# RWKV core stage: 26 products a round in place of 30, with wider ones, on sequences copied by GpSimd

## The reference, cut to what matters

```
def rwkv7_step(S, inp):
    r_t, dec_t, k_t, v_t, kk_t, a_t = inp
    sa = jnp.einsum('bhij,bhj->bhi', S, -kk_t)
    S = (S * dec_t[:, :, None, :]
         + sa[..., None] * (kk_t * a_t)[:, :, None, :]
         + v_t[..., None] * k_t[:, :, None, :])
    y = jnp.einsum('bhij,bhj->bhi', S, r_t)
    return S, y
```

## Time and profile before

| | |
|---|---|
| median of 3 runs | 2794.38 us (2792.1 to 2809.73) |
| the profiled execution | 2812.66 us, its span 2810.9 us |
| PE busy | 2584.5 us of the span (92%), 26234 matmuls |
| DVE, ACT, POOL busy | 1440.3, 1164.2, 947.7 us |
| core stage | 281.3 to 505.0 us: 223.7 us, PE busy 171.9 us |

### The profile page before, as it was taken

One profiled execution on the slowest core, in us unless ns is written; L12 is line 12 of the kernel. 1 busy time (PEld: TensorE's weight loads), 2 busy tenths in 40 slices (PEclk: granted clock), 3 DMA queues, 4 the chain that ended last, 5 costly groups with the idle time before them and its releaser, 6 DMA issues.

```text
span 2810.9 us, 64105 instructions
## 1 busy us (share of the span) xinstructions
PE 2584.5 (92%) x26234; PEld 2414.1 (86%) x26234; DVE 1440.3 (51%) x2006; ACT 1164.2 (41%) x1683; POOL 947.7 (34%) x392
## 2 busy tenths in 40 slices
PE   6797777798999999999899999999999899999997
PEld 5776777488799999988697999999998758999997
DVE  7827444421267774389654677743143234655521
ACT  7732333444343443333544434434246533543432
POOL 2232000044144445433441444444442202444442
PEclk8798999999999999999999999999999889999999
DMA  3121000124122223322221223233222101222231
GB/s 136 61 68 49 16 4 5 65 84 141 46 83 97 90 90 106 124 79 82 91 91 43 85 97 97 90 106 113 89 90 68 46 0 54 97 90 95 99 103 63
DMA packets 61128, 219.96 MB, mean 78 GB/s; under 512 B 6688, under 2 KB 7072, under 8 KB 60320
## 3 DMA queue, kind: packets, MB, share of 16 engines
q1 hardware_dynamic: 57536, 206.43, 21.8%
q10 hardware_dynamic: 3424, 11.01, 1.0%
HBM read 213.22 MB, written 4.19 MB: 77 GB/s over the span
## 4 chain that ended last, share of the span: by engine, by line
PE 64%; issue 22%; DVE 8%; POOL 3%; ACT 3%; DVEq 0%; POOLq 0%; ACTq 0%
PE psum L501 58%; DVE psum L2270 5%; POOL wl L486 3%; PE psum L878 1%; PE psum L921 1%; PE psum L1096 1%; PE psum L1095 1%; DVE tmp L1896 0%; DVE fox_max L2463 0%; PE psum L1118 0%; ACT wh L1186 0%; DVE fox_p L2488 0%; PE psum L909 0%; PE psum L1098 0%; PE psum L544 0%
## 5 line engine op out<-in xcount | busy, mean ns | idle before, releaser
L486 POOL TENSOR_TENSOR wl<-raw,wh 128x1024 fp32r<-128x1024 f32 x388 | 947.5, 2447 | 1830.2 <-ACT wh L1186 1828.9
L501 PE MATMUL psum<-acth,wh 128*128 128x256 f32 x3792 | 769.7, 285 | 42.0 <-DVE actl L1853 15.8
L501 PE MATMUL psum<-actl,wh 128*128 128x256 f32 x3792 | 757.5, 281 | 0.0
L501 PE MATMUL psum<-acth,wl 128*128 128x256 f32 x3792 | 757.1, 281 | 0.0
L501 PEld LDWEIGHTS psum<-acth,wh 128*128 128x128 f32 x3792 | 584.8, 190 | 61.8 <-issue 40.2
L1186 ACT ACTIVATE wh<-raw 128x1024 fp32r<-128x1024 f32 x388 | 407.3, 1056 | 535.5 <-PE psum L501 532.7
L501 PEld LDWEIGHTS psum<-actl,wh 128*128 128x128 f32 x3792 | 586.4, 190 | 0.0
L501 PEld LDWEIGHTS psum<-acth,wl 128*128 128x128 f32 x3792 | 585.3, 190 | 0.0
L2200 DVE TENSOR_TENSOR cu<-psum,rstd 128x512 f32<-128x512 f32 x132 | 91.1, 690 | 242.8 <-PE psum L501 228.1
L501 PE MATMUL psum<-hidh,wh 128*128 128x256 f32 x1056 | 205.8, 276 | 0.0
L501 PE MATMUL psum<-hidl,wh 128*128 128x256 f32 x1056 | 205.5, 276 | 0.0
(11 more groups left out here) (414 smaller groups left out, 4218.3 us busy)
## 6 DMA issues: line engine op xcount, KB each, us to landing
raw<-in_weights SPq DMA_DIRECT2D x388, 512.0 KB, 3.4
xt<-in_x SPq DMA_DIRECT2D x4, 512.0 KB, 5.4
xt<-in_x ACTq DMA_DIRECT2D x1, 2048.0 KB, 9.2
out_x<-xt ACTq DMA_DIRECT2D x4, 512.0 KB, 3.0
mem<-in_mem ACTq DMA_DIRECT2D x1, 1024.0 KB, 11.0
memn<-memh ACTq DMA_DIRECT2D x1, 1024.0 KB, 3.9
memn<-meml ACTq DMA_DIRECT2D x1, 1024.0 KB, 6.8
memh<-memn ACTq DMA_DIRECT2D x1, 1024.0 KB, 5.4
```

The lines of the kernel that those rows point to most:

```text
L486: pool.tensor_tensor(wl[:, s, :], raw[:, s, :], wh[:, s, :].bitcast(F32), ALU.subtract).then_inc(split_done, 1)
L501: ins = pe.matmul(out[:, n:n + HALF], w, m[:, n:n + HALF], start=first and n == 0, stop=last and n + HALF >= out.shape[1])
```

## The change

1. The five sequences become one tensor `seqs`, at the same addresses. GpSimd copies what a chunk needs into fixed buffers: WR (w and r of chunk c), WA (w and a of the chunk after next), WRE (w, r and an identity beside them), AK (a and k), VS (v). That is 12 copies a round with a semaphore `core_s`; the hardware loop over weight units is cut in two, 32 units ahead of the core stage and the rest behind it.
2. Products with the same weights become one matmul over a wider moving operand. AM is a times (r, identity), 64x2x64, for CC and half of VB. KM is k times (w, r, identity), 64x3x64, for BE and K; v times the identity stays apart. M4 takes T1 and M together, 64x2x64. So 30 products become 26, with the same columns in all.
3. Every buffer of the core stage is single in place of alternating. AN is therefore written by DVE to AN_NEXT, and ACT copies it to AN (a new 128x512 copy for each g and round).
4. Order: CC moves from the head of a round into AM beside TT; N goes with M8, Y follows M8 and N, and S follows T4; KM stands before Z; BE's masks wait until ACT has copied KM's k and v parts; T64 stands alone at the round's end.

```diff
-        seq = {n: place("seq_" + n, [P, 16, 4, CH]) for n in "wakr"}
-        v_at = cursor[0]
-        seq["v"] = place("seq_v", [P, 16, 4, CH])
+        seqs = place("seqs", [P, 5, 16, 4, CH])
+        seq = {n: seqs[:, j] for j, n in enumerate("wakrv")}
+        v_at = cursor[0] - 16384
...
+        ND, AN0, CC, AT, TF, XX, UU, SS, VS = (both(n, 4) for n in ("nd", "an", "cc", "at", "tf", "x", "u", "s", "vs"))
+        T1M, TBZ, WRE = both("t1m", 3, 4), both("tbz", 3, 4), both("wre", 4, 3)
+        AN_NEXT, AN, BE, KTV, WA, WR, AK = (both(n, 2, 4) for n in ("an_next", "an12", "be", "ktv", "wa", "wr", "ak"))
...
+            def core_stage(i, c, n):
+                if c:
+                    for g in range(2):
+                        if c > 1:
+                            pool.wait_ge(core_in[g], when(IN_AT, "Y", i, -1))
+                        pool.tensor_copy(WR[g][:, :, :, :], seqs[:, 0:4:3, i + 8 * g, :, :]).then_inc(core_s[g], 1)
+                if n > 1:
+                    for g in range(2):
+                        pool.wait_ge(core_x[g], when(X_AT, "N", i, 1))
+                        pool.tensor_copy(WA[g][:, :, :, :], seqs[:, 0:2, i + (8 * g + 2), :, :]).then_inc(core_s[g], 1)
+                if n:
+                    for g in range(2):
+                        if c:
+                            pool.wait_ge(core_in[g], when(IN_AT, "KM", i, 0))
+                        for j in range(2):
+                            pool.tensor_copy(WRE[g][:, :, j, :], seqs[:, 3 * j, i + (8 * g + 1), :, :])
+                        pool.tensor_copy(AK[g][:, :, :, :], seqs[:, 1:3, i + (8 * g + 1), :, :])
+                        pool.tensor_copy(VS[g][:, :, :], seqs[:, 4, i + (8 * g + 1), :, :]).then_inc(core_s[g], 1)
+            pool.sem_inc(split_done, UC)
+            with pool.Fori(0, LOWS_FIRST) as i:
+                weight_lows(i)
+            pool.wait_ge(prep_done, 5 + 1)
+            pool.wait_ge(evacuated, plan("v", "tile") + 8 + UC)
+            pool.wait_ge(ccore_in, 16)
+            for g in range(2):
+                pool.tensor_copy(WRE[g][:, :, 2, :], ident64.rearrange("p (o t) -> p o t", o=1).to_broadcast([P, 4, CH]))
+            core_stage(-1, 0, 2)
+            for i in range(NCH - 2):
+                core_stage(i, 2 if i else 1, 2)
+            core_stage(NCH - 2, 2, 1)
+            core_stage(NCH - 1, 2, 0)
+            with pool.Fori(LOWS_FIRST, UNITS // SLOTS) as i:
+                weight_lows(i)
...
-            def core_cc(g, c, q):
-                done(core_in, g, q, inside(q, slot(g, 3, 0), tok("a", g, c), tok("r", g, c)))
...
-            def core_m4(g, n, q):
-                M_, MT = of(MM[g][0][:, 0]), of(MM[g][0][:, 1])
-                inside(q, slot(g, 0, 0), MT, of(T1[g][n % 2]))
-                inside(q, slot(g, 1, 0), MT, M_)
-                done(core_in, g, q, inside(q, slot(g, 1, 1), M_, MT))
...
-            def core_vb(g, n, q):
-                inside(q, slot(g, 2, 0), tok("v", g, n), eye)
-                done(core_in, g, q, inside(q, slot(g, 2, 1), tok("a", g, n), eye))
...
-            def core_be(g, n, q):
-                inside(q, slot(g, 3, 0), tok("k", g, n), tok("w", g, n))
-                done(core_in, g, q, inside(q, slot(g, 3, 1), tok("k", g, n), tok("r", g, n)))
...
-            def core_k(g, n, q):
-                done(core_in, g, q, inside(q, slot(g, 2, 0), tok("k", g, n), eye))
...
+            def core_am(g, q):
+                done(core_in, g, q, inside(q, slots(g, 2), of(AK[g], 0), lambda q: WRE[g][:, q, 1:3, :]))
+            def core_km(g, q):
+                inside(q, split_slots(g, 0, 3), of(AK[g], 1), lambda q: WRE[g][:, q, :, :])
+                done(core_in, g, q, inside(q, split_slots(g, 3, 4), of(VS[g]), eye))
...
+            def core_m4(g, q):
+                inside(q, slots(g, 0), of(T1M[g], 2), lambda q: T1M[g][:, 0:2, q, :])
+                done(core_in, g, q, inside(q, slot(g, 1, 0), of(T1M[g], 1), of(T1M[g], 2)))
...
+            def core_round(i, c, n):
+                for g in range(2):
+                    if c:
+                        pe.wait_ge(core_s[g], when(POOL_AT, "WR", i, 0))
+                        pe.wait_ge(core_v[g], when(DVE_AT, "BE", i, 0))
+                        pe.wait_ge(core_a[g], when(ACT_AT, "KM", i, 0))
+                    else:
+                        pe.wait_ge(core_v[g], when(DVE_AT, "N", i, 1))
+                    for q in range(4):
+                        if n:
+                            core_m2(g, q)
+                        if c:
+                            core_x_(g, q)
+                for g in range(2):
+                    if c:
+                        pe.wait_ge(core_v[g], when(DVE_AT, "T64", i, 0))
+                    if n:
+                        pe.wait_ge(core_a[g], when(ACT_AT, "M2", i, 1))
+                        core_m4(g, 0)
+                        core_m4(g, 1)
+                    if c:
+                        pe.wait_ge(core_a[g], when(ACT_AT, "X", i, 0))
+                    for q in (2, 3):
+                        if n:
+                            core_m4(g, q)
+                        if c:
+                            core_u(g, 2 * q - 4)
+                            core_u(g, 2 * q - 3)
+                for g in range(2):
+                    if n:
+                        pe.wait_ge(core_a[g], when(ACT_AT, "M4", i, 1))
+                        pe.wait_ge(core_v[g], when(DVE_AT, "M4", i, 1))
+                    if n > 1:
+                        pe.wait_ge(core_s[g], when(POOL_AT, "WA", i, 2))
+                    for q in range(4):
+                        if n:
+                            core_m8(g, q)
+                        if n > 1:
+                            core_n(g, q, of(WA[g], 1), of(WA[g], 0))
+                    if c:
+                        pe.wait_ge(core_a[g], when(ACT_AT, "U", i, 0))
+                        for q in range(4):
+                            core_y(g, q)
+                if not n:
+                    return
+                for g in range(2):
+                    pe.wait_ge(core_a[g], when(ACT_AT, "M8", i, 1))
+                    pe.wait_ge(core_v[g], when(DVE_AT, "M8", i, 1))
+                    for q in range(4):
+                        core_t4(g, q)
+                    if c:
+                        for q in range(4):
+                            core_s_(g, q)
+                for g in range(2):
+                    if c:
+                        pe.wait_ge(core_a[g], when(ACT_AT, "Y", i, 0))
+                        pe.wait_ge(core_v[g], when(DVE_AT, "S", i, 0))
+                    else:
+                        pe.wait_ge(core_v[g], when(DVE_AT, "T4", i, 1))
+                    pe.wait_ge(core_s[g], when(POOL_AT, "SB", i, 1))
+                    for q in range(4):
+                        core_tt(g, q)
+                        core_am(g, q)
+                for g in range(2):
+                    pe.wait_ge(core_a[g], when(ACT_AT, "TT", i, 1))
+                    for q in range(4):
+                        core_t32(g, q)
+                for g in range(2):
+                    pe.wait_ge(core_v[g], when(DVE_AT, "CC", i, 1))
+                    pe.wait_ge(core_a[g], when(ACT_AT, "AM", i, 1))
+                    core_km(g, 0)
+                    core_km(g, 1)
+                    pe.wait_ge(core_v[g], when(DVE_AT, "T32", i, 1))
+                    for q in (2, 3):
+                        core_km(g, q)
+                        core_z(g, 2 * q - 4)
+                        core_z(g, 2 * q - 3)
+                for g in range(2):
+                    pe.wait_ge(core_a[g], when(ACT_AT, "Z", i, 1))
+                    for q in range(4):
+                        core_t64(g, q)
...
+                        act.wait_ge(core_v[g], when(DVE_AT, "N", i, 1))
+                        act.activation(wide(AN[g]), wide(AN_NEXT[g]), ACT.Identity).then_inc(core_a[g], 1)
...
+                for g in range(2):
+                    act.wait_ge(core_x[g], when(X_AT, "Z", i, 1))
+                    core_evac(g, TBZ[g][:, 2, :, :], 1, 0, 256)
+                for g in range(2):
+                    act.wait_ge(core_in[g], when(IN_AT, "KM", i, 1))
+                    act.activation(KTV[g].rearrange("p j (b q) t -> p b j (q t)", b=2),
+                                   psum[:, 4 * g + 2:4 * g + 4, 256:512].rearrange("p b (j t) -> p b j t", j=2),
+                                   ACT.Identity).then_inc(core_a[g], 1)
...
+            def core_decays_end(g, back):
+                dve.tensor_tensor(AN_NEXT[g][:, 1, :, :], quarter(bank[4 * g + 3], 1), every(m_a[:, 2, :]), mul)
+                chain.wait(back)
+                dve.tensor_tensor(T1M[g][:, 0, :, :], ND[g][:, :, :], every(ident64), add).then_inc(core_v[g], 1)
...
+                    dve.wait_ge(core_a[g], when(ACT_AT, "KM", i, 1))
+                    for j in range(2):
+                        ins = dve.tensor_tensor(
```

(37 more changed lines are left out.)

362 lines of the change are left out of this document (139 added, 223 removed).

## The result

The changed kernel takes 2787.97 us (median of 20 runs, 2781.32 to 2795.59) against 2804.67 us for the kernel before in its 20 runs (2792.1 to 2813.03). The ratio is 0.9941, 95% interval 0.993 to 0.9952: 0.6% or 16.7 us faster, within 1%, as forecast (18 us).

The account below looks back on a forecast made before the run. PE's instruction fetch (3.73 us per 127 matmul records) bounds the core stage. A steady round of 24.2 + 0.9 + 0.5 = 25.6, say 25.5 us, plus smaller gains in the other rounds, gives 18 us less: 2776 us, range 2763 to 2796.

Parts of the forecast that it names:

- The fetch as the bound: Core stage: PE paced by instruction fetch, 3.73 us per 127 matmul records; 7.2 fewer blocks, 27 us less at full pace.
- The fourth rival: Core stage: no effect; stops come from PE's own products, whose columns stay; 2 us less, 2792 us; chance 0.04.
- the rule that spoke for it: Skill's instruction fetch section: next page fetched during execution, 16 KiB crossings mostly hidden, so fewer instructions would be worth nothing.
- PE's own work: Core stage: each dropped matmul pair saves 5 ns; 464 pairs, 2 us, only where PE's work decides.
- (a): Round's end: KM's copy follows Z's copies, then BE's masks; M2 starts 1.9 us later, PE idle 0.6 to 1.1 us.
- (b): Block holding KM, Z and T64 takes 4.6 us, 0.9 over its fetch; together with (a) 0.9 us a round.
- (c): New copy AN on ACT, 0.60 us twice a round, between U and M8: covered by the other g's work, costs nothing.
- DVE held by GpSimd: Core stage: DVE operations with two SBUF inputs (T1, S * keep) held by GpSimd's copies; 0.5 us a round, 0 to 2.4.
- The third rival: GpSimd's queue of 12 copies bounds the round, from 6.1 ns an element on; slower, 2856 us at 8 ns; chance 0.04.
- The weight units: Unit 32's low part and SP's reload move to some 25 us before the core stage's end; reader comes later: nothing.
- Rival 2: Core rounds: hand-overs eat the gain, adding 2.4 us a round or more beyond the fetch; 2785 to 2796 us; chance 0.22.
- Rival 1: Core stage: full gain, every block stays at its fetch; 27 us less, 2767 us; chance 0.14.

Follow-up runs that it names:

- e1_narrow: Changed kernel with its three wide products (AM, KM, M4) split again, 30 products a round for 26; 2818.31 us, ratio 1.0022 to the kernel before.
- e2_loop: Changed kernel with PE running the six full core rounds as a hardware loop; 2783.93 us, ratio 0.9894 to the kernel before.
- e7_wide: Changed kernel with 64 unused columns added to M8's first product and T4, no more instructions; 2790.83 us, ratio 0.9917 to the kernel before.
- e8_loop_wide: e2_loop with the added unused columns of e7_wide; 2790.89 us, ratio 0.9951 to the kernel before.
- e3_act_order: Changed kernel with ACT copying KM of g = 0 before Z of g = 1; 2790.96 us, ratio 0.9923 to the kernel before.
- e4_pool_twice: Changed kernel with every GpSimd copy in the core stage made twice, first into a spare buffer; 2793.15 us, ratio 0.9941 to the kernel before.
- r1_after_again: Changed kernel run and profiled again unaltered (the second profile); 2789.18 us, ratio 0.9929 to the kernel before.
- e5_loop_narrow: e2_loop with the products split as in e1_narrow, a loop body of about 124 KB; 2847.22 us, ratio 1.0149 to the kernel before.
- e6_loop_order: e2_loop with the ACT copy order of e3_act_order; 2774.45 us, ratio 0.9899 to the kernel before.

## Why the prediction was right, point by point

**The fetch as the bound: right, and now shown.** By its own step the count was to fall by 7.2 blocks (6592 records), with q8 at 51 or 52 packets. Both came. The price of a block, 3.73 us from the trace of before, is 3.5 us in e1_narrow. (The sum took 128 records a block for 58.7 and 51.5 and 127 elsewhere, which shifts the difference by 0.1 block.) The fourth rival and the rule that spoke for it (The Trainium skill, "Runtime: NRT & Kernel Launch", section "Instruction fetch mechanics": mostly hidden) fall with e1_narrow, e2_loop and the pair e7_wide and e8_loop_wide: in straight code of short fp32 matmuls a block cost about 0.8 us of standstill (47.2 us over 59 blocks before the change).

**PE's own work: right in the sum, wrong in the part.** The prediction had 2 us less in the stage, at 5 ns for each dropped pair; PE busy is 171.5 us for 171.9. But e1_narrow has 11.3 us more than the changed kernel for 512 pairs. About 2 us of that are its two stretches at 1.2 GHz (an estimate: some 100 records took 3.4 us in each, and would take 2.3 to 2.4 at the rate of the rounds around them); that leaves 18 ns a pair. The dropped pairs saved more than reckoned, and the new order gave it back. The runs don't show where; KM's four columns' worth on one half of PE, where K and BE had stood beside products of the other half, is the likely place. It decided nothing, since work below the block's length is free (e7_wide).

**The round's end, (a) and (b): the mechanism right, the size too large.** The step took 0.9 us a round. The steady round is 24.57 us against the bare fetch's 24.2, in the second profile 24.8, so 0.4 to 0.6 us for everything on top; e1_narrow against the kernel before says 0.3. The wait for BE was there as described (0.6 us in each of seven stops), and e3_act_order took it away without shortening the round: most of it lay inside the fetch. With (c), AN's copy at nothing, no run quarrels: it appears in no wait over 0.3 us.

**DVE held by GpSimd: mis-sized.** The step took 0.5 us a round from 2.35 ns an element. Measured are 1.2 ns, and of 14 lengths of S * keep one over 1 us (1377 ns); e4_pool_twice, at twice the load, has full rounds as long as r1_after_again's, to within what two profiles can tell. The nearest row, a subtraction of two inputs, was no good measure for a copy of one. This and the point before are why the round came out at 24.6 to 24.8 and not at 25.5 us. The third rival needed 6.1 ns an element and was far off.

**The weight units: the step said "Nothing", and named the wrong cover.** It looked only at the reader of the weights, which indeed didn't wait. It left out that the reload is a transfer in a stage whose bound is another transfer. In the first profile that cost 2.07 us and took most of the gain of the last stretch, in the second nothing.

**Opening and last stretch.** Forecast were 1 us for the opening, 2.0 for the seventh round and 0.5 for the last. The last two together gave 1.4 us in one profile, with the stop of 2.07 in it, and 3.5 in the other (33.42 for 32.00 and 29.90). The opening gave 0.8.

**The sum.** In the stage 18 us were forecast and 21.1 measured. The two steps on the cost side were 0.7 to 0.9 us a round too large together, which makes 4 to 5 us more gain, and the reload's 2.07 us take a part back. The 27.95 us a round that the sum started from were 0.25 too long, by the late cut; what the rounds lose by that (1.5 us) the last stretch gains, and the stage as a whole is not touched. By the medians it is 16.7 us. The profiled executions lay 8.0 and 1.5 us over their medians, which is just the difference (23.2 less 6.5); how much of the 8.0 us lies in the core stage of before isn't settled, and so the medians alone can't tell 18 from 21. The predicted 2776 us stands on the three runs shown (median 2794.38), and the twenty runs of the same kernel, those three among them, have 2804.67: the measured 2788 lies 12 us above the forecast, of which 10 are that and 1 the size of the gain. Rival 2 had its middle at 2789 us, so by the time alone it looks right; it is not. It wanted 2.4 us a round beyond the fetch, a gain of 5 us, and rounds of 26.6; measured are 0.4 to 0.6 us and 24.6 to 24.8. That 2788 lies in the stated range owes something to the range's width: the baseline alone was off by 10 us. Rival 1, the full gain, would have needed 24.2 us in every round.

## What to carry to other kernels

Where PE runs straight code of short matmuls, look in the trace for stops at even counts of instructions and for the packets of its instruction queue: if a block's work is shorter than its fetch, only fewer fetched instructions help, and columns, copies and short waits are free up to the fetch. There a wider product is worth what it saves in instructions. A loop whose body stays on the chip takes away the fetches that are left (here a further 6.6 us in the stage, where the change gave 21.1); a body slightly too long is worse than no loop. After such a change ask what else moves data at that time.

## What the runs showed of the hardware that was not expected

- A PE loop body of 107 KB of instructions ran five turns with no fetch; one of 124 KB was fetched anew each turn, with a stop of 3.6 to 4.1 us at the jump back and rounds of 33.6 us, where straight code of the same products takes 28.6.
- A 0.5 MB load into SBUF that met a fetch of instructions delayed it by about 2.5 us (6.2 us from one fetch to the next, for 3.5 to 3.8), and by about 1.7 in e5_loop_narrow (5.5 us), with stops of PE of 2.07 and 2.36 us.
- GpSimd copies fp32 within SBUF at 0.61 us for 128x512 and 0.40 for 128x256, 1.2 ns an element at the larger size, against 2.35 ns for its subtraction.
- A DVE operation with two SBUF inputs waited 3.08 us, through five GpSimd copies without a gap between them.
- The fastest kernels of the study are the loops, e2_loop and e6_loop_order: 1.1% and 1.0% faster than the kernel before (2783.93 and 2774.45 us in batches whose medians of before were 2811.96 and 2803.32), where the change alone gives 0.6 to 0.7%.
